# Filter quarters six units sooner with their inputs first, and filter taps formed on two row halves, in a hybrid HGRN2/Hyena layer

## The chip, the cores and the metric

The kernel runs on one core of one Trainium2 chip. The metric is the device time of one execution in microseconds (us). A core has five engines that run their own instruction streams beside each other and meet at semaphores: TensorE (PE), VectorE (DVE), ScalarE (ACT), GpSimd (POOL) and SyncE (SP, here the issuer of most DMAs). The times of the kernel before are 3018.55, 3019.62 and 3019.79 us, median 3019.62 us.

## The reference, cut to what matters

One layer of a diffusion backbone over 256 latent tokens `x` and 256 context tokens, 2048 wide, float32. In this order: a SwiGLU feed-forward network (FFN) for both streams; a mixer, half of it a gated recurrence and half a long two-sided convolution; a second FFN; a final norm. Two preparations stand ahead of the first FFN. The conditioning (`mx`, `mc`: shift, scale and gate vectors) is a product of two vectors with an 18432-column matrix:

```python
mx = [m[:, None, :] for m in jnp.split(jax.nn.silu(c) @ ada_w[l] + ada_b[l], N_MOD, axis=-1)]
mc = jnp.split(jax.nn.silu(c_ctx) @ ada_w[l] + ada_b[l], N_MOD, axis=-1)
x = x + 0.5 * mx[2] * _swiglu(_modulate(_rmsnorm(x, norm_ffn1[l]), mx[0], mx[1]),
                              ffn1_w1[l], ffn1_w3[l], ffn1_w2[l])
```

And the filters of the convolution, from a small network over the 256 positions, through a Fourier transform:

```python
hid = jnp.sin(freq * (z @ w1 + b1))
hid = jnp.sin(freq * (hid @ w2 + b2))
hid = jnp.sin(freq * (hid @ w3 + b3))
h = (hid @ w_out).reshape(n, 2, 2, HY_WIDTH)
...
h = h * jnp.exp(-t[:, None] * deltas)[:, None, None, :]
h_fwd = h[:, :, 0]
h_bwd = h[1:, :, 1]
l1 = jnp.sum(jnp.abs(h_fwd), axis=0) + jnp.sum(jnp.abs(h_bwd), axis=0)
filt = jnp.concatenate([h_fwd, jnp.zeros((1, 2, HY_WIDTH), F32), h_bwd[::-1]], axis=0) / l1
return jnp.fft.rfft(filt, axis=0)
```

The transform needs only the sum and the difference of the forward and the backward taps.

## The kernel before

Weights of the FFNs, the mixer and the output projection stream through in tiles of 128 x 1024 float32 (512 KB). Each is split by ACT (`w_hi`, L431) and DVE (`w_lo`, L438) into two parts, and PE multiplies three times (`three_pass`, L448 to L450). From about 100 us on, this is what the kernel does to its end. The change touches the part ahead of it, which is written out by hand as one loop on each engine over steps `o` from 0 to `TAIL`.

**Conditioning units.** The 4096 columns of `ada_w` that the first norm needs are fetched as 64 units of 128 x 1024 (`load_wide`, L698) on SP's queue. PE takes unit `o` in step `o` with two narrow matmuls (`unit`, L1354: two of the four 32-column strips of the array; the next unit has the other two). Each unit lands in a place of the list `LAND`; the load of a later unit into that place waits until PE has taken the earlier one (`cond_used`). The first 40 units have 16 places, units 40 to 63 have six. In between, SP loads the context tokens `yin`, the decay `window`, the transform `dft` and, at the units of `FIRST_LOADS_AT`, the first FFN weight tiles (L406).

**The filter.** Three layers of the small network are at steps `LAYER_AT` (PE, L1329; seven DVE operations L2089 to L2107; the sine on ACT, L1704). Then come four quarters of 512 filter channels, started at the steps `SPEC_AT`. A quarter goes: POOL's queue loads `fout`, the forward weights on rows 0 to 63 and the backward weights on rows 64 to 127 (L1230); `raw_taps` makes sum and difference for 128 positions at a time (L1381), each as one matmul over all 128 rows, from `hid_sum` and from `hid_dif`, which is `hid_sum` with the sign of its first half turned by `signs`; DVE multiplies by the window (L2124); `spectra` transforms (L1402); ACT and DVE fold even and odd parts (L1735, L2131, L2133) and ACT's queue writes 512 KB twice (`spill`, L1740); `absolute`, `tabs_sum`, `l1_norm` (L1393) and `inverse` make the L1 norm.

**The tokens.** `tokens` turns x and the context with matmuls against the identity (L1340), ACT copies them (L1709) and squares them for the norm. `to_columns` (L1367) and `take` finish a set of 16 units; after the second, DVE and ACT make the FFN's input, one block of 128 columns at a time (`scaled1`, `low1`, L521 and L532; L552), from step `MOD_FIRST` on.

**The opening of the FFN.** After step `TAIL - 1` the first weight tile's matmuls begin (`col_unit`). Its tile has four groups `k` of six matmuls; `inside(j, k)` puts the remaining units 48 to 63 between the groups of tiles `j` = 0 to 3, and the last `l1_norm` and two `to_columns` as well.

Line numbers are those of the kernel before.

Of the kernel before, what the change touches and what calls it, by code (L numbers as in the profile page):

```python
# [23 lines left out]
P = 128  # L24
# [62 lines left out]
SPEC_AT = (10, 18, 28, 36)  # L87
# [9 lines left out]
def shape_tables():  # L97
# [25 lines left out]
    window = blocks(np.exp(-tt[:, None] * deltas)[by_parity]).astype(np.float32)  # L123
# [32 lines left out]
def build(nc, i, out):  # L156
    with ExitStack() as life:
# [64 lines left out]
        fout = sb("fout", [P, 512], scope=first)  # L222
        hid = [sq_sum[:, n * SEQ:(n + 1) * SEQ] for n in range(2)]
        hid_sum = sb("hid_sum", [P, SEQ], scope=first)
        hid_dif = sb("hid_dif", [P, SEQ], scope=first)
        hid.append(hid_sum[:])
# [429 lines left out]
        FIRST_LOADS_AT = (39, 41, 45, 50, 56, 62)  # L656
# [559 lines left out]
        def _(po):  # L1216
# [7 lines left out]
            def filter_out(q):  # L1224
                filt, half = q // 2, q % 2
                if q:
                    po.wait_ge(fs_taps_pe, 4 * q)
                for r in range(2):
                    c0 = filt * (2 * HY) + r * HY + half * 512
                    po.dma_start(fout[r * FILT_ORDER:(r + 1) * FILT_ORDER, :], i["filt_w_out"][0][:, c0:c0 + 512]).then_inc(fs_in, 16)  # L1230

            filter_out(0)
            for q in range(1, 4):
                filter_out(q)

# [44 lines left out]
        MLP_SMALL = 16 * 11  # L1280
# [4 lines left out]
        SQUARES_AT, SUM_AT, ROOT_AT, DIAG_AT, NORM_AT, SPREAD_AT = (5, 5, 7, 7, 11, 11, 12, 12), 14, 14, 15, 24, 25  # L1285
# [4 lines left out]
        WINDOW_AT = ((11, 13), (19, 21), (29, 31), (37, 38))  # L1290
# [1280 lines left out]
```

## Time and profile before

| | us |
|---|---|
| median of three runs | 3019.62 |
| profiled execution, its own time | 3019.63 |
| its span (first to last instruction) | 3017.8 |
| PE busy in the span | 2969.1 |
| DVE busy | 2049.1 |
| ACT busy | 1160.7 |
| POOL busy | 147.7 |
| start of the first FFN matmul | 101.97 |

The profile is of one execution. Times in its rows count from the start of the span, and 1.8 us of the execution lie outside the span. A busy time is the time in which an engine had an instruction running; a wait is the idle time in front of an instruction, with what ended it behind `<-`. PEclk is the granted TensorE clock, 1.00 at the upper of its two levels (2.4 GHz), 0.50 at the lower (1.2 GHz). A row of the timeline with x8 is eight records of one kind in a row: a float32 matmul leaves two, so a pair of units leaves eight and a single unit four.

### The profile page before, as it was taken

The page shows a single profiled execution, that of the slowest core. Times are in us where ns is not written, and L with a number is a line of the kernel's source. Part 1 is how long each engine was busy: PE and PEld are TensorE (multiplying, and loading weights), DVE is VectorE, ACT ScalarE, POOL GpSimd, SP SyncE. Part 2 cuts the span into 40 slices and gives each one's busy share as a digit, 9 for nine tenths or more (in the row PEclk, how much of TensorE's full clock was granted, in tenths as well). Part 3 has the DMA queues.
Part 4 walks back from the last instruction along what each step waited for, and adds up shares of the span by engine and source line. Part 5 has one row for each costly group of instructions (what it writes and reads, how often), then busy time and mean ns, then how long its engine had stood idle before and what let it go on. Part 6 is the DMA issues. An engine that isn't in the chain of part 4 may idle for free. (4 is left out here: it accounts for less than half of the span.)

```text
span 3017.8 us, 42600 instructions
## 1 busy us (share of the span) xinstructions
PE 2969.1 (98%) x15878; PEld 2528.7 (84%) x15878; DVE 2049.1 (68%) x2663; ACT 1160.7 (38%) x1477; POOL 147.7 (5%) x181
## 2 busy tenths in 40 slices
PE   7999999999999999999999999999999999999998
PEld 3588888888888888888889999999998888888886
DVE  4598667676766677673477767778866666666667
ACT  4332222222222222222248777754345444444444
POOL 1000000000000000000000033430000000000001
PEclk9999999999999999999999999999999999999999
DMA  9965546354466758563345554555565666666664
GB/s 370 327 209 188 181 134 202 128 178 146 157 221 221 255 168 282 186 228 102 95 98 167 171 166 148 153 152 180 158 203 168 188 192 190 188 193 189 189 193 147
DMA packets 369856, 559.07 MB, mean 185 GB/s; under 512 B 18175, under 2 KB 260216, under 8 KB 368840
## 3 DMA queue, kind: packets, MB, share of 16 engines
q1 hardware_dynamic: 364112, 544.62, 56.6%
q0 software_dynamic: 2640, 8.52, 0.9%
q10 hardware_dynamic: 2984, 4.29, 0.4%
q8 instruction: 80, 1.31, 0.2%
q14 instruction: 40, 0.33, 0.0%
HBM read 551.06 MB, written 6.30 MB: 185 GB/s over the span
## 5 line engine op out<-in xcount | busy, mean ns | idle before, releaser
L438 DVE TENSOR_TENSOR w_lo<-raw,w_hi 128x1024 fp32r<-128x1024 f32 x736 | 912.6, 1242 | 677.4 <-ACT w_hi L431 675.9
L431 ACT ACTIVATE w_hi<-raw 128x1024 fp32r<-128x1024 f32 x736 | 777.5, 1059 | 1484.2 <-PE bank L450 1093.6
L684 DVE SCALAR_TENSOR_TENSOR states<-ada_raw,silu_c,states 128x1024 f32<-128x1024 f32 x300 | 375.4, 1280 | 2.3
L448 PE MATMUL bank<-h_hi_early,w_hi 128*128 128x512 f32 x768 | 300.7, 391 | 1.0 <-issue 1.0
L450 PE MATMUL bank<-h_hi_early,w_lo 128*128 128x512 f32 x768 | 298.9, 389 | 0.0
L449 PE MATMUL bank<-h_lo_early,w_hi 128*128 128x512 f32 x768 | 298.8, 389 | 0.0
L448 PE MATMUL bank<-hx_hi,w_hi 128*128 128x256 f32 x1024 | 295.2, 288 | 0.0
L450 PE MATMUL bank<-hx_hi,w_lo 128*128 128x256 f32 x1024 | 289.6, 283 | 0.0
L449 PE MATMUL bank<-hx_lo,w_hi 128*128 128x256 f32 x1024 | 289.6, 283 | 0.0
L454 PE MATMUL bank<-w_hi,h 128*128 128x512 f32 x736 | 287.7, 391 | 1.9 <-DVE h L532 1.3
L456 PE MATMUL bank<-w_lo,h 128*128 128x512 f32 x736 | 286.5, 389 | 0.0
L455 PE MATMUL bank<-w_hi,h 128*128 128x512 f32 x736 | 286.4, 389 | 0.0
L448 PE MATMUL bank<-h_hi_late,w_hi 128*128 128x512 f32 x704 | 274.0, 389 | 0.0
L450 PE MATMUL bank<-h_hi_late,w_lo 128*128 128x512 f32 x704 | 273.9, 389 | 0.0
L449 PE MATMUL bank<-h_lo_late,w_hi 128*128 128x512 f32 x704 | 273.9, 389 | 0.0
L448 PE MATMUL bank<-g_hi,w_hi 128*128 128x512 f32 x640 | 249.1, 389 | 0.0
L450 PE MATMUL bank<-g_hi,w_lo 128*128 128x512 f32 x640 | 249.0, 389 | 0.0
L449 PE MATMUL bank<-g_lo,w_hi 128*128 128x512 f32 x640 | 249.0, 389 | 0.0
L449 PEld LDWEIGHTS bank<-hx_lo,w_hi 128*128 128x128 f32 x1024 | 196.3, 192 | 0.2
L448 PEld LDWEIGHTS bank<-hx_hi,w_hi 128*128 128x128 f32 x1024 | 196.2, 192 | 0.2
L450 PEld LDWEIGHTS bank<-hx_hi,w_lo 128*128 128x128 f32 x1024 | 196.1, 191 | 0.0
L1007 DVE SCALAR_TENSOR_TENSOR x_res<-bank,gate,x_res 128x256 f32<-128x256 f32 x176 | 84.8, 482 | 147.7 <-PE bank L450 147.4
(341 smaller groups left out, 4815.0 us busy)
## 6 DMA issues: line engine op xcount, KB each, us to landing
raw<-in_ffn_w_dram SPq DMA_DIRECT2D x528, 512.0 KB, 4.1
ada_raw<-in_ada_w_dram SPq DMA_DIRECT2D x252, 512.0 KB, 4.5
raw<-in_w_in_dram SPq DMA_DIRECT2D x176, 512.0 KB, 3.8
raw<-in_w_out_dram SPq DMA_DIRECT2D x32, 512.0 KB, 3.6
ada_ahead<-in_ada_w_dram SPq DMA_DIRECT2D x20, 512.0 KB, 16.3
raw<-in_ada_w_dram SPq DMA_DIRECT2D x8, 512.0 KB, 18.7
ada_more<-in_ada_w_dram SPq DMA_DIRECT2D x8, 512.0 KB, 8.0
spec<-spec_spill POOLq DMA_DIRECT2D x8, 512.0 KB, 4.0
```

The source lines that it names most:

```text
L431: nc.scalar.activation(w_hi[un.slot(j)][:], raw[un.slot(j)][:], ACT.Copy).then_inc(hi_done, 1)
L438: nc.vector.tensor_tensor(w_lo[un.slot(j)][:], raw[un.slot(j)][:], w_hi[un.slot(j)][:].bitcast(F32), ALU.subtract).then_inc(lo_done, 1)
L448: nc.tensor.matmul(o, w_hi[slot][:, c0:c0 + P], hi, start=start, stop=False, skip_group_check=True)
L449: nc.tensor.matmul(o, w_hi[slot][:, c0:c0 + P], lo, start=False, stop=False, skip_group_check=True)
L450: return nc.tensor.matmul(o, w_lo[slot][:, c0:c0 + P], hi, start=False, stop=stop, skip_group_check=True)
L454: nc.tensor.matmul(o, hi, w_hi[slot][:, c0:c0 + 512], start=start, stop=False, skip_group_check=True)
L455: nc.tensor.matmul(o, lo, w_hi[slot][:, c0:c0 + 512], start=False, stop=False, skip_group_check=True)
L456: return nc.tensor.matmul(o, hi, w_lo[slot][:, c0:c0 + 512], start=False, stop=stop, skip_group_check=True)
L684: nc.vector.scalar_tensor_tensor(out=total, in0=src, scalar=silu_c[:, m, t:t + 1], in1=total, op0=ALU.mult, op1=ALU.add).then_inc(done, 1)
L1007: ins = nc.vector.scalar_tensor_tensor(out=part[:, d, :], in0=bank[downs[d % len(downs)]][:, t * 256:(t + 1) * 256], scalar=gate[:, gt, d, ...
```

## The change

1. `SPEC_AT` goes from (10, 18, 28, 36) to (4, 14, 22, 30). All follow-up steps of a quarter now stand at fixed distances from it. The three layers go from steps 2, 4, 8 to -4, -2 and 1, so the first two stand ahead of unit 0. The tokens of x go to steps 0 and 1, those of the context to 12 and 13.
2. On SP's queue the inputs of the first layers (`emb`, `fw1`, and the three parts of `fw23`, till now on ACT's queue) go ahead of `xin`; `window` and `dft` go behind unit 1, and `yin` behind unit 9.
3. `TAIL` goes from 48 to 44: the FFN opens behind unit 43, and 20 units stand inside it (`INSIDE`), two more pairs between the groups of the first two tiles. `MOD_FIRST` goes from 37 to 35, and the FFN's first weight loads from units (39, 41, 45, 50, 56, 62) to (36, 40, 45, 51, 56, 61). The last `l1_norm` goes from inside the FFN to step 38.
4. POOL loads both halves of a quarter's weights on rows 0 to 63 (`fout_raw`) and makes their sum on rows 0 to 63 of `fout` and their difference on rows 64 to 127. `raw_taps` multiplies the sum by the upper and the difference by the lower 64 rows of one `hid_sum`: two matmuls of 64 rows each in place of two of 128. `signs` goes. The window's first row is halved on the host's table, and DVE makes the one position that has no backward tap with two operations on one partition per quarter.

```diff
-SPEC_AT = (10, 18, 28, 36)
+SPEC_AT = (4, 14, 22, 30)
...
-    window = blocks(np.exp(-tt[:, None] * deltas)[by_parity]).astype(np.float32)
+    decay = np.exp(-tt[:, None] * deltas)
+    decay[0] *= 0.5
+    window = blocks(decay[by_parity]).astype(np.float32)
...
-        FIRST_LOADS_AT = (39, 41, 45, 50, 56, 62)
+        FIRST_LOADS_AT = (36, 40, 45, 51, 56, 61)
...
+            sy.dma_start(emb[:], i["t_emb"]).then_inc(c_in, 16)
+            sy.dma_start(fw1[:], i["filt_w1"][0]).then_inc(c_in, 16)
+            sy.dma_start(fw23[:, 0, :], i["filt_w2"][0]).then_inc(mlp_in, 16)
+            for r in range(2):
+                sy.dma_start(fw23[:, 1 + r, :], i["filt_w3"][0]).then_inc(mlp_in, 16)
             sy.dma_start(xin[:], i["x"][0].rearrange("(a p) d -> p a d", p=P)).then_inc(x_in, 16)
-            for g in range(4):
-                load_wide(sy, g)
-            sy.dma_start(yin[:], i["ctx"][0].rearrange("(a p) d -> p a d", p=P)).then_inc(y_in, 16)
-            for g in range(4, 8):
+            for g in range(2):
                 load_wide(sy, g)
             sy.dma_start(window[:].rearrange("p a c -> p (a c)"), i["t_window"]).then_inc(window_in, 16)
             sy.dma_start(dft[:], i["t_dft"]).then_inc(window_in, 16)
-            for g in range(8, 10):
+            for g in range(2, 10):
                 load_wide(sy, g)
+            sy.dma_start(yin[:], i["ctx"][0].rearrange("(a p) d -> p a d", p=P)).then_inc(y_in, 16)
...
+            def both_ways(q):
+                po.wait_ge(fs_in, 32 * (q + 1))
+                po.wait_ge(*((fs_taps_pe, 4 * q) if q else (memsets, 4)))
+                nc.gpsimd.tensor_tensor(fout[0:FILT_ORDER, :], fout_raw[:, 0, :], fout_raw[:, 1, :], ALU.add).then_inc(fs_hid, 1)
+                po.wait_ge(fs_hid, 2 * q + 1)
+                nc.gpsimd.tensor_tensor(fout[FILT_ORDER:P, :], fout_raw[:, 1, :], fout_raw[:, 0, :], ALU.subtract).then_inc(fs_hid, 1)
...
-        LAYER_AT, ANGLES_AT, SINE_AT = (2, 4, 8), (2, 4, 8), (4, 7, 11)
-        TOKENS_AT, EVICT_AT = (4, 4, 6, 6, 8, 8, 10, 10), (4, 4, 6, 6, 8, 8, 10, 10)
+        LAYER_AT, ANGLES_AT, SINE_AT = (-4, -2, 1), (-4, -2, 1), (-3, -1, 2)
+        TOKENS_AT, EVICT_AT = (0, 0, 1, 1, 12, 12, 13, 13), (0, 0, 1, 1, 12, 12, 13, 13)
...
-        TAIL = 48
-        L1_AT, INVERSE_AT = (20, 28, 37), (21, 29, 38)
...
-        MOD_FIRST = 37
-        FIRST_ROUND_AT = (41, 43, 45)
...
+        TAIL = 44
+        L1_AT, INVERSE_AT = (12, 22, 30, 38), (13, 23, 31, 39)
+        MOD_FIRST = 35
+        FIRST_ROUND_AT = (39, 41, 43)
+        INSIDE = {(0, 0): 44, (0, 1): 46, (0, 2): 48, (1, 0): 50, (1, 1): 52, (1, 2): 54, (2, 0): 56, (2, 2): 58, (3, 0): 60, (3, 2): 62}
...
-                pe.wait_ge(fs_in, 32 * (q + 1))
-                pe.wait_ge(fs_hid, 3)
-                for n, both in enumerate((hid_sum, hid_dif)):
-                    nc.tensor.matmul(bank[2 * a + n][:], both[:, a * P:(a + 1) * P], fout[:], start=True, stop=True
+                    pe.wait_ge(fs_taps, 6 * q)
+                pe.wait_ge(fs_hid, 2 * q + 2)
+                for n in range(2):
+                    own = slice(n * FILT_ORDER, (n + 1) * FILT_ORDER)
+                    nc.tensor.matmul(bank[2 * a + n][:], hid_sum[own, a * P:(a + 1) * P], fout[own, :], start=True, stop=True
...
+                if a == 0:
+                    ve.wait_ge(fs_taps, 6 * q + 2)
+                    nc.vector.tensor_tensor(tsum[0:1, 0, :], tsum[0:1, 0, :], tdif[0:1, 0, :], ALU.subtract).then_inc(fs_taps, 1)
+                    ve.wait_ge(fs_taps, 6 * q + 3)
+                    nc.vector.tensor_scalar(tdif[0:1, 0, :], tsum[0:1, 0, :], -1.0, None, ALU.mult).then_inc(fs_taps, 1)
```

SP's queue, from the third load of the program on; `rows` and `ident` are small inputs, `fw` the layers' weights, L698 and L700 the conditioning units. Before:

```order
L1161 DMA ident<-in_t_ident_dram 128x128
L1162 DMA xin<-in_x_dram 128x2x2048
L698 DMA ada_raw<-in_ada_w_dram 128x1024 x4
L1165 DMA yin<-in_ctx_dram 128x2x2048
L698 DMA raw<-in_ada_w_dram 128x1024 x4
L1168 DMA window<-in_t_window_dram 128x2048
L1169 DMA dft<-in_t_dft_dram 128x512
```

Now:

```order
L1163 DMA ident<-in_t_ident_dram 128x128
L1164 DMA emb<-in_t_emb_dram 33x256
L1165 DMA fw<-in_filt_w_dram 33x64
L1166 DMA fw<-in_filt_w_dram 64x64
L1168 DMA fw<-in_filt_w_dram 64x64 x2
L1169 DMA xin<-in_x_dram 128x2x2048
L700 DMA ada_raw<-in_ada_w_dram 128x1024 x2
L1172 DMA window<-in_t_window_dram 128x2048
L1173 DMA dft<-in_t_dft_dram 128x512
L700 DMA ada_raw<-in_ada_w_dram 128x1024 x2
```

Five small loads stand between `ident` and `xin`; `yin` follows eight units later.

PE at the opening of the FFN (L1354 and L1360 are the units, four rows a pair; L448 to L450, now L450 to L452, the matmuls of a group, of which the first three stand here). Before, from unit 44 on:

```order
L1354 MATMUL bank<-ada_more,c_wide 32x512 x4
L1354 MATMUL bank<-ada_raw,c_wide 32x512 x4
L448 MATMUL bank<-h_hi_early,w_hi 128x512
L449 MATMUL bank<-h_lo_early,w_hi 128x512
L450 MATMUL bank<-h_hi_early,w_lo 128x512
...
L1354 MATMUL bank<-ada_raw,c_wide 32x512 x4
```

Now, from unit 40 on:

```order
L1360 MATMUL bank<-ada_raw,c_wide 32x512 x8
L450 MATMUL bank<-h_hi_early,w_hi 128x512
L451 MATMUL bank<-h_lo_early,w_hi 128x512
L452 MATMUL bank<-h_hi_early,w_lo 128x512
...
L1360 MATMUL bank<-ada_more,c_wide 32x512 x4
```

Units 44 and 45 (`ada_more`) stood two pairs ahead of the first group and now stand behind it; 46 and 47 follow behind the second.

PE around the first filter quarter (L1381 and L1387 are its taps, L1340 and L1346 the tokens, L1329 and L1333 the layers). Before:

```order
L1354 MATMUL bank<-ada_raw,c_wide 32x512 x4
L1329 MATMUL bank<-emb,fw 64x256
L1354 MATMUL bank<-ada_raw,c_wide 32x512 x4
L1329 MATMUL bank<-sq_sum,fw 64x256
L1340 MATMUL bank<-ident,xin 128x128 x16
```

Now:

```order
L1333 MATMUL bank<-emb,fw 64x256
L1333 MATMUL bank<-sq_sum,fw 64x256
L1346 MATMUL bank<-ident,xin 128x128 x16
L1360 MATMUL bank<-ada_raw,c_wide 32x512 x2
L1333 MATMUL bank<-sq_sum,fw 128x256
L1346 MATMUL bank<-ident,xin 128x128 x16
L1360 MATMUL bank<-ada_raw,c_wide 32x512 x6
L1387 MATMUL bank<-fout,sq_sum 128x512 x2
```

The first two layers now stand ahead of every unit, and the first taps (the last row) behind four units instead of ten.

## Rows read from the trace of the kernel before

**Rows 1.** Busy time in the span, the page's first part.
```profile
PE 2969.1 (98%) x15878; PEld 2528.7 (84%) x15878; DVE 2049.1 (68%) x2663; ACT 1160.7 (38%) x1477; POOL 147.7 (5%) x181
```

**Rows 2.** Stretches: length, busy of each engine, granted clock, DMA share, GB/s.
```profile
60.00:80.00 20.00, 20.00 (x98) 7.48 (x99) 12.09 (x44) 6.99 (x9) 1.67 (x4) 1.00 1.04 377
80.00:100.00 20.00, 17.14 (x77) 5.01 (x77) 17.48 (x35) 7.53 (x16) 0.00 (x0) 1.00 1.04 395
100.00:120.00 20.00, 18.41 (x94) 10.26 (x94) 12.16 (x23) 8.33 (x12) 0.00 (x0) 1.00 1.03 396
140.00:160.00 20.00, 20.00 (x94) 16.67 (x93) 18.34 (x41) 9.91 (x19) 0.00 (x0) 1.00 0.43 147
```

**Rows 3.** PE timeline, first 40 us: start, length, form, idle before.
```profile
18.36 1.11 PE L1329 MATMUL bank<-emb,fw 33*64 33x256 f32 x2 [0.58 <-DMA fw<-in_filt_w_dram]
28.21 1.97 PE L1340 MATMUL bank<-ident,xin 128*128 128x128 f32 x16
35.23 1.06 PE L1354 MATMUL bank<-ada_ahead,c_wide 128*32 128x512 f32 x8
```

**Rows 4.** PE timeline, 40 to 102 us.
```profile
40.19 1.84 PE L1381 MATMUL bank<-fout,hid_sum 128*128 128x512 f32 x2 [1.99 <-DVE hid_dif L2114]
...
44.71 1.12 PE L1381 MATMUL bank<-fout,hid_sum 128*128 128x512 f32 x2
...
46.62 1.06 PE L1354 MATMUL bank<-ada_ahead,c_wide 128*32 128x512 f32 x8
47.62 1.98 PE L1402 MATMUL bank<-tsum,dft 128*128 128x512 f32 x4
49.53 1.06 PE L1354 MATMUL bank<-ada_ahead,c_wide 128*32 128x512 f32 x8
...
99.56 1.05 PE L1354 MATMUL bank<-ada_raw,c_wide 128*32 128x512 f32 x4 [1.71 <-DMA ada_raw<-in_ada_w_dram]
```

**Rows 5.** PE timeline, opening of the FFN.
```profile
101.97 0.50 PE L448 MATMUL bank<-h_hi_early,w_hi 128*128 128x512 f32 x1
...
103.56 1.05 PE L1354 MATMUL bank<-ada_raw,c_wide 128*32 128x512 f32 x4
...
109.84 1.06 PE L1354 MATMUL bank<-ada_more,c_wide 128*32 128x512 f32 x8 [1.00 <-DMA ada_more<-in_ada_w_dram]
...
115.71 0.50 PE L448 MATMUL bank<-h_hi_early,w_hi 128*128 128x512 f32 x1
...
117.22 0.95 PE L1367 MATMUL bank<-pairs,states 128*128 128x4 f32 x8
```

**Rows 6.** SP's queue: issue time and length of the issue.
```profile
1.68 0.41 SPq L1161 DMA_DIRECT2D ident<-in_t_ident_dram  x1
2.13 0.43 SPq L1162 DMA_DIRECT2D xin<-in_x_dram  x1
...
81.97 0.94 SPq L698 DMA_DIRECT2D ada_raw<-in_ada_w_dram  x2
...
102.08 0.33 SPq L698 DMA_DIRECT2D ada_raw<-in_ada_w_dram  x1
```

**Rows 7.** Issues at 82 us, at 102 us, and the spills: KB, median us to landing.
```profile
ada_raw<-in_ada_w_dram SPq DMA_DIRECT2D x2, 512.0 KB, 11.3
...
ada_raw<-in_ada_w_dram SPq DMA_DIRECT2D x1, 512.0 KB, 10.3
...
spec_spill<-spec_cos ACTq DMA_DIRECT2D x4, 512.0 KB, 8.1
```

**Rows 8.** Stretches, columns as in the second group: near the start; two at lower clock.
```profile
3.00:4.00 1.00, 0.16 (x1) 0.16 (x1) 0.00 (x0) 0.00 (x0) 1.00 (x3) 1.00 0.76 137
5.00:6.00 1.00, 0.00 (x0) 0.00 (x0) 0.00 (x0) 0.00 (x0) 1.00 (x3) 1.00 0.94 385
40.40:43.80 3.40, 3.40 (x8) 0.86 (x11) 0.71 (x2) 3.38 (x7) 0.00 (x0) 0.50 1.04 413
1560.00:1570.00 10.00, 7.50 (x50) 7.53 (x51) 9.66 (x22) 6.65 (x13) 0.00 (x0) 0.83 0.23 61
```

**Rows 9.** DVE and POOL operations of the quarters' shape.
```profile
L2139 DVE TENSOR_TENSOR tabs<-tabs x4: 692/692/693, 52.9 to 108.9; 128x512 f32<-128x512 f32 x4
...
L1276 POOL TENSOR_TENSOR xt<-x_tok,norm_row 128x512 f32<-128x512 f32 x7 | 10.9, 1552 | 798.2 <-DVE x_tok L1033 798.2
```

More of the change, by code:

```diff
@@ L222, in build @@
         fout = sb("fout", [P, 512], scope=first)
+        fout_raw = sb("fout_raw", [FILT_ORDER, 2, 512], scope=first)
         hid = [sq_sum[:, n * SEQ:(n + 1) * SEQ] for n in range(2)]
-        hid_sum = sb("hid_sum", [P, SEQ], scope=first)
-        hid_dif = sb("hid_dif", [P, SEQ], scope=first)
-        hid.append(hid_sum[:])
+        hid_sum = hid[0]
+        hid.append(hid_sum)
         ada_more = [sb(f"ada_more{n}", [P, UNIT], scope=first) for n in range(2)]
@@ L1226, in filter_out @@
                 if q:
-                    po.wait_ge(fs_taps_pe, 4 * q)
+                    po.wait_ge(fs_hid, 2 * q)
                 for r in range(2):
                     c0 = filt * (2 * HY) + r * HY + half * 512
-                    po.dma_start(fout[r * FILT_ORDER:(r + 1) * FILT_ORDER, :], i["filt_w_out"][0][:, c0:c0 + 512]).then_inc(fs_in, 16)
-            filter_out(0)
-            for q in range(1, 4):
+                    po.dma_start(fout_raw[:, r, :], i["filt_w_out"][0][:, c0:c0 + 512]).then_inc(fs_in, 16)
+            def both_ways(q):
[4 more added lines that the diff above has]
+                nc.gpsimd.tensor_tensor(fout[FILT_ORDER:P, :], fout_raw[:, 1, :], fout_raw[:, 0, :], ALU.subtract).then_inc(fs_hid, 1)
+            for q in range(4):
                 filter_out(q)
+                both_ways(q)
             po.wait_ge(mod_done, 12)
@@ L1314, in turn @@
             def turn(n, after):
-                pe.wait_ge(after, 48 if n == 3 else SMALL)
+                pe.wait_ge(after, 80 if n == 3 else SMALL)
                 if n < 3:
@@ L1336, in tokens @@
                     pe.wait_ge(tr_out, g - 3)
+                if g == 8:
+                    pe.wait_ge(fs_out, 4)
                 for k in range(2):
@@ L1406, in _ @@
             pe.wait_ge(memsets, 3)
-            for o in range(TAIL):
+            for o in range(LAYER_AT[0], TAIL):
                 if o in LAYER_AT:
@@ L1430, in _ @@
                     l1_norm(L1_AT.index(o))
-                unit(o)
+                if o >= 0:
+                    unit(o)
             def inside(j, k):
-                g = TAIL + 4 * j + k
-                if k in (0, 2) and g < ADA_UNITS:
-                    unit(g)
-                    unit(g + 1)
-                if (j, k) == (0, 3):
-                    l1_norm(3)
+                if (j, k) in INSIDE:
+                    unit(INSIDE[j, k])
+                    unit(INSIDE[j, k] + 1)
                 if (j, k) == (1, 1):
@@ L1691, in _ @@
                                  ).then_inc(mlp_in, 16)
-            ac.dma_start(fw23[:, 0, :], i["filt_w2"][0]).then_inc(mlp_in, 16)
-            for r in range(2):
-                ac.dma_start(fw23[:, 1 + r, :], i["filt_w3"][0]).then_inc(mlp_in, 16)
             ac.wait_ge(cols_done, 1)
@@ L1715, in square_tokens @@
                 if n >= 2:
-                    ac.wait_ge(n1["sq"], n - 1)
-                nc.scalar.activation((sq2 if n % 2 else xn2)[:], src, ACT.Square, accum_out=tok_sq[:, n:n + 1]).then_inc(n1["sq"], 1)
+                    ac.wait_ge(n1["sq"], n if n >= 4 else n - 1)
+                nc.scalar.activation((sq2 if n in (1, 3) else xn2)[:], src, ACT.Square, accum_out=tok_sq[:, n:n + 1]
+                                     ).then_inc(n1["sq"], 1)
             def row_out(nth):
@@ L1740, in spill @@
                 ac.dma_start(dst, spec_out[o][:]).then_inc(fs_dma[o], 16)
-            for o in range(TAIL):
+            for o in range(LAYER_AT[0], TAIL):
                 if o in SINE_AT:
@@ L2169, in scaled1 @@
                 scaled(ve, n1, 0, [x_res, y_res], (0, 1), kb)
-            for o in range(TAIL):
+            for o in range(LAYER_AT[0], TAIL):
                 if o in ANGLES_AT:
@@ L2180, in _ @@
                     lanes()
-                if o == SPEC_AT[0]:
-                    signs()
                 if o in TAKE_AT:
```

62 lines of the change are left out of this document (21 added, 41 removed).

## The prediction, written before the changed kernel was run

> **What bounds the kernel now.** I read the busy times first. PE has an instruction running in 2969.1 of 3017.8 us [rows 1], so the end moves only by what PE's waits or its work lose or gain. Then the stretches. From 140 us on PE is busy throughout and the DMA engines have spare time (share 0.43); from 60 to 120 us the DMA share is full and PE nearly so [rows 2]. The reader is to see two nearly equal bounds side by side there: PE's instruction stream and the stream of loads. The PE timeline tells which one ends last. Up to 95 us PE takes units long after they have landed. From unit 44 on it waits for them: 1.71 us before unit 46, and inside the FFN once more, 1.00 us before units 50 and 51, which landed at 109.8 [rows 4, 5]. So the opening of the FFN is set by PE's earlier work up to 95 us, and by the stream just behind it. SP's queue comes last: units 42 and 43 are issued at 82 us and take 11.3 us to land, at about 94; unit 53 is issued at 102.08 and takes 10.3, to 112.4 [rows 6, 7]. A full queue stands in front of each, so bandwidth and not the issue sets these times.
>
> The profiled execution took 3019.63 us, as good as the median of 3019.62. The sum is made on it.
>
> **What PE saves.** Eight calls of `raw_taps`: with the clock up, one call holds PE from 44.71 to 46.62, 1.91 us, for two matmuls of the full height [rows 4]. On two row halves with two banks they can run side by side, 0.95 us a call: 7.6 us. If they don't, 0. The nearest row for the better end is the pair of units: four matmuls on four column strips take 1.0 us (46.62 to 47.62), about as long as one unit alone (four records, 1.05 us) [rows 4], so the array does run strips at once. I take 0.95.
>
> The Trainium skill (TensorEngine Tiling (Array Packing), Key Properties) says that row tiles work in parallel, but also that each change of the tiling mode drains TensorE, and now two kinds of tiling alternate with full-height work. The trace agrees that this is cheap: the pair of units and the full-height transform alternate at 1.00 and 1.91 us without a gap. By the rule a drain would be paid as before, since units and taps differed in mode already.
>
> The earlier start saves more. The first layer waited until 18.9 us for its weights, then the tokens and three layers followed, and the first taps began at 40.19 behind a wait of 1.99 for the signs [rows 3, 4]. In the new order the first taps stand behind four units and need only x.
>
> **When PE could open the FFN.** Put the context tokens as PE's new start. They stand behind unit 11. In front of that in the stream stand x, 12 units, window, dft and yin, the same bytes as before in front of unit 11; unit 9 was taken as it landed at 35.2 [rows 3], so unit 11 about 2.6 later, 37.8. With the shift worked out below 39.3, and one unit more, 40. From there to the FFN PE has: tokens 2 x 1.97, 32 units at 0.5 (16.0), six calls of taps (5.7), six transforms at 1.91 (11.5), four `l1_norm`, two `to_columns` and the norm at 1.0 (7), together 44: ready at 84. Without the side by side 90. DVE's two added operations on one partition have at most the length of a full one, 0.69 us [rows 9]: 1.4 a quarter, 5.5 in all, less 0.6 for `signs`. They lie between taps and transform; if nothing covers them PE is ready 4 us later, 88 (94). POOL's two operations have 64 rows; for 128 rows of the same length one took 1.55 [rows 9], so 3.1 a quarter at most. Behind the last taps of a quarter follow at least six units and two transforms, 6.8 us, before the next taps: covered. For the first quarter nobody waits before 25 us.
>
> **When the stream opens it.** Five small loads stand in front of `xin` now. Successive issues there are 0.45 us apart (1.68, 2.13) [rows 6], so x is issued up to 2.25 later. Before, the engines were partly used in that time (0.76 in the fourth microsecond, 0.94 in the sixth) [rows 8], and the small loads fall into it, moved from ACT's queue. Bounds of the shift: 0 and 2.25; I take 1.5, nearer the upper, since x is most of what ran there. From then on the engines are full until past 110, and the shift stays. In front of unit 43 stand two FFN loads, as before; but the last quarter's two spills of 512 KB now come in front of it as well. At 395 GB/s [rows 2] that is 1.33 each, 2.7. Unit 43 lands at 94.1 + 1.5 + 2.7 = 98.3, and a unit takes 1.0: the FFN opens at 99.3. PE would be ready at 84 to 94, so the stream decides, and the 7.6 us of the taps become waiting.
>
> **Inside the FFN.** A group takes 1.4 us, 1.6 behind a unit (101.97 to 103.56) [rows 5]. Up to unit 53 there are now six groups and five pairs: 9.2 + 5.0 = 14.2, which gives 113.5. But unit 53 lands at 112.4 + 1.5 = 113.9 (all spills and as many FFN loads, four, stand in front of it in both kernels), so its matmuls end at 114.95. What comes next is `to_columns`, in both kernels behind six groups and unit 53; it stood at 117.22 [rows 5]. `l1_norm` has been done on both sides. Gain 117.22 - 114.95 = 2.27 us. From there the order is the same in both, the later units landed more than 2.3 us ahead of their use, and PE had no wait up to 160 but one: the gain goes through to the end. 3019.63 - 2.3 = 3017.3 us.
>
> So of 7.6 us saved in matmuls and more than 10 in an earlier start, 2.3 arrive.
>
> **Rivals.**
>
> A. The stream isn't shifted, or runs denser because PE frees its places sooner. For: the small loads fill a gap that was there. Against: share 1.04 between 80 and 120 already [rows 2]. Unit 53 at 112.4 gives 117.22 - 113.45 = 3.8: 3015.8. A stream that is also 1.5 us denser gives 5.3: 3014.3.
>
> B. The lower clock. PE is now idle for about a third of the time between 40 and 98. Before, the idle 1.99 us at 38 to 40 was followed by 3.4 us at clock 0.50 [rows 4, 8], in which taps took 3.5 instead of 1.9. If such a stretch falls on the first groups of the FFN, half of its work, 1.7 us, is lost: 3019.0. While PE only waits for units it costs nothing.
> The Trainium skill (TensorE: Matmul & The Clock Gate, Part 1) says that the lower clock is the default and only activity releases it; by this rule more waiting means more such stretches, and the sum with one is the 3019.0 just worked out.
> Further on there are such stretches too, as at 1560 to 1570 with mean 0.83 [rows 8]; each holds 1.7 us, and whether short waits there bring one may change with any shift, to both sides.
>
> C. Slower: PE is the bound after all. Place: the hand-overs of a quarter, PE taps, DVE window, PE transform, ACT, DVE, PE's next taps. The taps that covered DVE's work are halved and DVE has 1.4 us more. It decides from an opening of the FFN at 117.22 - 14.2 = 103.0 on, and each microsecond later costs one. Against: PE's 84 leaves 19 us, and the loop before ran from 44 to 95 without a wait. With 24 hand-overs (three quarters of eight) of 1 us each it is 108: 3024.6.
>
> D. The row halves don't run side by side. For: no row shows row halves. PE is ready at 90 to 94, still before 98: the time stays 3017.3. This rival shows only in the spacing of the taps, and I give it a fifth of the chance of the forecast.
>
> E. The loads in front of x hold the stream more than issue time, because x's packets queue behind many tiny ones. From a shift of 3.8 on the kernel is slower; 5 would give 3020.8.
>
> **Chances.** Forecast, D included: 0.60. A 0.17 (of it 0.05 beyond 0.2%, with a later low-clock stretch gone as well: 3014.3 - 1.7 = 3012.6). B 0.12. C 0.07, of it 0.05 slower by over 0.2%. E 0.04, of it 0.02. A measurement of this kernel tells 0.2%, 6.0 us, from no change; 2.3 us lies within. So faster 0.05, within 0.88, slower 0.07. The forecast's own range is 3015.8 (shift 0) to 3019.0 (one low-clock stretch); the range for 8 in 10 goes to A's denser stream, 3014.2, and to E's 3020.8.
>
> **What would show it.** Right: first taps at about 25 us; a call of taps in about 1 us; waits of PE for units all along 45 to 98, 10 us or more in sum; the FFN opening at 99 +- 2 behind a load, with short waits for units inside; `to_columns` of the third set at about 115; the same from 140 on, shifted. Wrong: if PE's waits before the FFN name DVE or ACT, it is C; if x lands later than 14.5, E; if unit 53 is taken well before 112, A's stream is denser than I believe; if the difference arises behind 160 us, none of this is the cause.

## The result, and the profile after

The changed kernel takes 3028.53 us (median of 8 runs, 3025.61 to 3031.68) against 3019.70 (3017.82 to 3020.23) for the kernel before on the same chip: ratio 1.0031, 95% interval 1.0021 to 1.0040. It is slower by 8.8 us. 3017.3 was forecast, in a range up to 3020.8. The profiled run took 3025.61, the lowest of the eight, and its span is 6.0 us longer than before's, so the rows show 6.0 of the 8.8 us.

The page's first part has PE's own work smaller, as intended: 2965.1 us where [rows 1] has 2969.1. The span grew all the same.

```profile
span 3023.8 us, 42617 instructions
PE 2965.1 (98%) x15878; PEld 2526.5 (84%) x15878; DVE 2052.1 (68%) x2668; ACT 1162.3 (38%) x1477; POOL 157.8 (5%) x189
```

The stretches that answer to [rows 2], same columns:

```profile
60.00:80.00 20.00, 15.21 (x58) 5.80 (x58) 11.87 (x46) 4.77 (x8) 0.14 (x1) 0.80 0.95 359
80.00:100.00 20.00, 19.86 (x98) 6.32 (x96) 13.19 (x26) 7.48 (x11) 2.53 (x2) 0.95 0.70 244
100.00:120.00 20.00, 14.93 (x79) 6.63 (x80) 17.95 (x37) 9.89 (x19) 0.00 (x0) 0.91 1.03 398
140.00:160.00 20.00, 20.00 (x99) 15.16 (x92) 11.77 (x26) 8.41 (x15) 0.00 (x0) 1.00 0.61 202
```

PE idles 4.8 of 20 us from 60 to 80, where it had no gap; its clock is at 0.80 there; and from 80 to 100 the stream of loads, full before, has a share of 0.70. The PE timeline names the waits (answers to [rows 3 to 5]; L1387 taps, L1360 units, L1346 tokens, L1406 transforms, L1372 `to_columns`, L1397 `l1_norm`, L1424 the norm):

```profile
24.84 1.13 PE L1387 MATMUL bank<-fout,sq_sum 64*128 64x512 f32 x4
...
42.80 1.94 PE L1360 MATMUL bank<-ada_ahead,c_wide 128*32 128x512 f32 x8 [6.30 <-DMA ada_ahead<-in_ada_w_dram]
44.67 3.56 PE L1346 MATMUL bank<-ident,yin 128*128 128x128 f32 x16
...
52.81 1.13 PE L1387 MATMUL bank<-fout,sq_sum 64*128 64x512 f32 x4
53.87 1.06 PE L1360 MATMUL bank<-ada_ahead,c_wide 128*32 128x512 f32 x8
...
61.04 1.35 PE L1372 MATMUL bank<-pairs,states 128*128 128x4 f32 x8 [4.05 <-ACT states L1721]
62.26 3.34 PE L1406 MATMUL bank<-tsum,dft 128*128 128x512 f32 x4
...
76.29 2.08 PE L1424 MATMUL bank<-xn,ones_d 128*128 128x512 f32 x2 [3.75 <-DVE hy_cols L2143]
...
101.59 1.05 PE L1397 MATMUL bank<-pairs,tabs 128*128 128x1 f32 x8 [1.73 <-DVE tabs L2135]
...
104.28 3.31 PE L1360 MATMUL bank<-ada_raw,c_wide 128*32 128x512 f32 x16
111.07 0.47 PE L450 MATMUL bank<-h_hi_early,w_hi 128*128 128x512 f32 x1 [3.48 <-issue]
...
125.38 1.05 PE L1372 MATMUL bank<-pairs,states 128*128 128x4 f32 x8
```

Read it from the top. The first taps stand at 24.84 instead of 40.19 [rows 4], and a call of taps holds PE 1.06 us (52.81 to 53.87) instead of 1.91. Then PE waits for ACT, for DVE, for DVE, and the FFN opens at 111.07 instead of 101.97 [rows 5]. The third `to_columns` stands at 125.38 instead of 117.22, 8.2 us later. From 140 on PE is busy without a gap as before.

Why ACT was late at 61.04: its rows from 56 us on (L1714 squares of the context, L1755 the root, L1752 the Exp of the bounds, L1721 `row_out`).

```profile
56.30 1.06 ACT L1714 ACTIVATE xn<-yin 128x1024 f32<-128x1024 f32 x1
57.26 0.19 ACT L1714 ACTIVATION_READ_ACCUMULATOR xn<-yin 128x1 f32 x1
57.46 1.28 ACT L1755 ACT_TABLE_LOAD   x1
58.76 0.20 ACT L1755 ACTIVATE pairs<-pairs 128x4 f32<-128x4 f32 x1
58.98 1.28 ACT L1752 ACT_TABLE_LOAD   x1
60.27 0.23 ACT L1752 ACTIVATE lbe<-lbe 128x32 f32<-128x32 f32 x1
60.41 0.58 ACT L1721 ACTIVATE states<-bank 128x512 f32<-128x512 f32 x1
```

`row_out` needs only unit 15, done at 54.9. It stands in ACT's order behind four squares of the context (the first starts at 52.55, when the tokens are out; they last to 57.46) and behind two table loads. In the kernel before the same squares ran from 39.16 to 43.45, long ahead of it:

```profile
52.17 0.60 ACT L1723 ACTIVATE states<-bank 128x512 f32<-128x512 f32 x1 [0.39 <-issue]
```

The DVE timeline has the same twice (L2182 the sum of the squares, L2115 the window products, L2058 to L2053 the bounds and lane sums, L2143 the end of `inverse`, L440 `w_lo`):

```profile
57.48 0.16 DVE L2182 TENSOR_TENSOR pairs<-pairs 128x4 f32<-128x4 f32 x1 [8.19 <-ACT xn L1714]
57.56 0.69 DVE L2115 TENSOR_TENSOR tsum<-bank,window 128x512 f32<-128x512 f32 x1
...
70.91 0.17 DVE L2058 TENSOR_TENSOR lbt<-lbe 128x16 f32<-128x16 f32 x1
...
73.54 0.20 DVE L2053 COPY same_lane<-same_lane 128x64 f32<-128x64 f32 x1
73.65 0.68 DVE L2115 TENSOR_TENSOR tsum<-bank,window 128x512 f32<-128x512 f32 x1
...
76.12 0.12 DVE L2143 TENSOR_TENSOR hy_cols<-bank,cols 128x4 f32<-128x4 f32 x1
...
109.75 1.22 DVE L440 TENSOR_TENSOR w_lo<-raw,w_hi 128x1024 fp32r<-128x1024 f32 x1
```

The first taps of the second quarter were done at 53.9; their window products stand behind a sum that waits for ACT, and start at 57.56. From 70.91 to 73.65 24 small operations, 2.7 us, stand ahead of the third quarter's products and of the `inverse` that the norm waits for. At the end the first `w_lo` stands behind the chain of `h_lo` parts; it ends at 110.97, and the first FFN matmul waits for it (the 3.48 us that the row calls `issue`). PE's late progress also holds up the loads. SP's issues (start, length):

```profile
5.78 0.61 SPq L1169 DMA_DIRECT2D xin<-in_x_dram  x1
...
57.02 10.41 SPq L700 DMA_DIRECT2D ada_raw<-in_ada_w_dram  x4
85.17 0.33 SPq L700 DMA_DIRECT2D ada_ahead<-in_ada_w_dram  x1
```

Between 67.4 and 85.2 SP issues nothing: the next unit's place is free only when PE has taken the unit before it in that place. No wait of PE between 44.67 and the opening names a load, so no row shows that this gap cost time.

### The profile page after: what moved, and what is told of

It is laid out like the page before. It is cut to its first block and busy times, and to the rows that moved or that the text cites. A ratio compares the mean times of both kernels' runs of the same rounds, so it can differ in the third digit from the quotient of the medians.

```text
span 3023.8 us, 42617 instructions
## 1 busy us (share of the span) xinstructions
PE 2965.1 (98%) x15878; PEld 2526.5 (84%) x15878; DVE 2052.1 (68%) x2668; ACT 1162.3 (38%) x1477; POOL 157.8 (5%) x189
## 5 line engine op out<-in xcount | busy, mean ns | idle before, releaser
L440 DVE TENSOR_TENSOR w_lo<-raw,w_hi 128x1024 fp32r<-128x1024 f32 x736 | 912.4, 1242 | 678.1 <-ACT w_hi L433 675.7
L450 PE MATMUL bank<-h_hi_early,w_hi 128*128 128x512 f32 x768 | 300.6, 391 | 4.5 <-issue 4.5
L452 PE MATMUL bank<-h_hi_early,w_lo 128*128 128x512 f32 x768 | 298.9, 389 | 0.0
L450 PE MATMUL bank<-hx_hi,w_hi 128*128 128x256 f32 x1024 | 295.2, 288 | 0.0
L452 PE MATMUL bank<-hx_hi,w_lo 128*128 128x256 f32 x1024 | 289.6, 283 | 0.0
L450 PE MATMUL bank<-h_hi_late,w_hi 128*128 128x512 f32 x704 | 274.0, 389 | 0.0
L452 PE MATMUL bank<-h_hi_late,w_lo 128*128 128x512 f32 x704 | 273.9, 389 | 0.0
L450 PE MATMUL bank<-g_hi,w_hi 128*128 128x512 f32 x640 | 249.1, 389 | 0.0
L452 PE MATMUL bank<-g_hi,w_lo 128*128 128x512 f32 x640 | 249.0, 389 | 0.0
L450 PEld LDWEIGHTS bank<-hx_hi,w_hi 128*128 128x128 f32 x1024 | 196.2, 192 | 0.2
L452 PEld LDWEIGHTS bank<-hx_hi,w_lo 128*128 128x128 f32 x1024 | 196.1, 191 | 0.0
```

The source lines that it names most:

```text
L440: nc.vector.tensor_tensor(w_lo[un.slot(j)][:], raw[un.slot(j)][:], w_hi[un.slot(j)][:].bitcast(F32), ALU.subtract).then_inc(lo_done, 1)
L450: nc.tensor.matmul(o, w_hi[slot][:, c0:c0 + P], hi, start=start, stop=False, skip_group_check=True)
L452: return nc.tensor.matmul(o, w_lo[slot][:, c0:c0 + P], hi, start=False, stop=stop, skip_group_check=True)
```

## The experiments

Beside each changed kernel the kernel before ran on the same chip; ratios are to it, with their 95% intervals. Not all experiments ran on one chip, so they are compared by these ratios.

**Row halves alone, steps as before.** The kernel before, with `fout_raw`, `both_ways`, the row halves in `raw_taps` and the two one-partition operations.

> The kernel before with the row halves, GpSimd's additions and the halved window row alone (part 4), all steps and the load order as before. Theory H (hand-overs, lower clock and the recycled places of the units make PE late in the changed kernel; the row halves are harmless): the eight calls of taps shrink from 1.91 to about 1.05 us, PE reaches the last units sooner and waits there for the stream, which ended last by about 3 us in sum, so 0 to 3 us faster than before: 3016.7 to 3019.7. Rival R (the row halves or GpSimd's additions are the cause): most of the 9 us appears here, 3024 or more. Rival S (the load order is the cause): no change, 3019.7.

3019.65 us, ratio 1.0002 (0.9993 to 1.0012): no change. PE timeline:

```profile
66.80 1.06 PE L1363 MATMUL bank<-ada_ahead,c_wide 128*32 128x512 f32 x8 [2.33 <-DMA ada_ahead<-in_ada_w_dram]
...
97.48 1.06 PE L1363 MATMUL bank<-ada_more,c_wide 128*32 128x512 f32 x8 [0.84 <-DMA ada_more<-in_ada_w_dram]
100.19 3.16 PE L1363 MATMUL bank<-ada_raw,c_wide 128*32 128x512 f32 x8 [1.64 <-DMA ada_raw<-in_ada_w_dram]
103.28 0.56 PE L450 MATMUL bank<-h_hi_early,w_hi 128*128 128x512 f32 x1
```

The time saved in the taps turns into waits for units, and part of it into the lower clock (100.19: a pair of units in 3.16 us). GpSimd's sums cost nothing that the time shows. So the loss lies in the other part.

**The new steps alone.** The changed kernel with full-height taps, `hid_dif` and `signs`.

> The changed kernel with full-height taps from two copies of the last layer's output, as before (parts 1 to 3 without part 4). H: as late as the changed kernel or later, since the taps take 7.6 us more of PE, part of it where PE waits anyway: 3027 to 3034. R: back to the kernel before, 3018 to 3021. S: as the changed kernel, 3028.5.

3029.38 us, ratio 1.0034 (1.0022 to 1.0047): the whole loss. PE waits 2.33 us for `states`, 1.59 for `hy_cols` and 1.73 for `tabs`, and opens the FFN at 110.16. Halving the taps buys 0.0003 of the ratio here, within both intervals. With full-height taps to cover DVE's work and without DVE's two operations the same three waits stand there, two of them shorter: neither the shorter taps nor these operations are the cause of the loss.

**The context stream sooner.**

```diff
-            for g in range(2, 10):
+            for g in range(2, 4):
                 load_wide(sy, g)
             sy.dma_start(yin[:], ...)
+            for g in range(4, 10):
+                load_wide(sy, g)
```

> The changed kernel with the context tokens loaded behind unit 3, as before, instead of behind unit 9; all else as changed. H: the wait for units 10 and 11 stays, since the same bytes stand in front of unit 11; PE still starts the context tokens at step 12, so 0 to 2 us less than the changed kernel: 3026.5 to 3028.5. S (the late context holds everything up): the opening of the FFN comes back by 5 us or more, 3023 or less. R: no change.

3030.82 us, ratio 1.0037 (1.0023 to 1.0051): no cure. The wait for loads moves to 33.19 (7.16 us), the others stay (4.05 for `states`, 3.41 for `hy_cols`), and the FFN opens at 113.10. The place of the context's load is not the cause.

**The context's squares, sums and root later.**

```diff
-        SQUARES_AT, SUM_AT, ROOT_AT, DIAG_AT, ... = (2, 3, 3, 4, 13, 14, 14, 15), 15, 15, 16, ...
+        SQUARES_AT, SUM_AT, ROOT_AT, DIAG_AT, ... = (2, 3, 3, 4, 17, 18, 19, 20), 21, 21, 21, ...
-                if o == 16:
+                if o == 20:
                     ac.wait_ge(lb_dve, 3)
```

> The changed kernel with ScalarE's squares of the context moved from steps 13 to 15 to steps 17 to 20 and the token sums, root and reciprocals from 15 and 16 to 21, behind the first row of sums (step 17) and VectorE's window products of the second quarter. H: PE's wait of 4.05 us for ScalarE's row goes, and VectorE no longer holds the window products for 8 us; PE reaches step 26 about 4 us sooner, the places come free sooner: 3022 to 3026, 4 us less than the changed kernel. S and R: no change, 3028.5.

3025.44 us, ratio 1.0021 (1.0011 to 1.0030). The Exp of the bounds moved with them, as the second part of the edit shows. The wait for `states` is gone, but the next one grew:

```profile
72.84 2.08 PE L1424 MATMUL bank<-xn,ones_d 128*128 128x512 f32 x2 [5.82 <-DVE hy_cols L2143]
```

PE came there sooner (65.96 instead of 71.48 for the unit ahead of it) and DVE did not.

**DVE's small operations later as well.** On top of the last one; the norm one step later with it. (By the rows they are 24 in 2.7 us, not 30 in 3.7 as the expectation has it.)

```diff
-... = (2, 3, 3, 4, 17, 18, 19, 20), 21, 21, 21, 24, 25
+... = (2, 3, 3, 4, 17, 18, 19, 20), 21, 21, 21, 25, 26
-                if o == 22:
+                if o == 26:
                     bounds_rest()
                     lanes()
```

> The kernel of the run with the context's squares later, and besides DVE's 30 small operations of the bounds and the lane sums (3.7 us) four steps later, into a gap of DVE, and the norm's matmul one step later. Theory H (hand-overs): the wait of 5.8 us that PE had there for hy_cols goes, the low clock behind it too, 4 to 6 us sooner at the first FFN group (103 or less, against 107.8), time 3020 to 3022. Rival S (the stream decides): PE's wait comes back as a wait for units, the FFN opens at 106 or later, time 3024 to 3026.

3020.01 us, ratio 1.0004 (0.9995 to 1.0013). Some 8 of the 8.8 us are back with no matmul, load or sum changed; only places in ACT's and DVE's order moved. The wait of 5.82 is 1.30, and

```profile
102.25 0.65 PE L450 MATMUL bank<-h_hi_early,w_hi 128*128 128x512 f32 x1 [3.00 <-issue]
...
118.05 1.05 PE L1372 MATMUL bank<-pairs,states 128*128 128x4 f32 x8
```

**DVE's small operations alone.** The changed kernel with only that second step.

> The changed kernel with DVE's 30 small operations four steps later and the norm's matmul one step later, the context's squares left where they are. Theory H: the wait of 2.1 us for hy_cols and the low clock behind it go, the wait for states (4.05) stays; time 3023 to 3026. Rival (only the two together help, or ACT's queue is the whole cause): within 1 us of the changed kernel, 3027 to 3029.

3022.82 us, ratio 1.0012 (1.0003 to 1.0021), better than expected. The wait for `hy_cols` is gone, the one for `states` (4.05 at 61.00) stays, the FFN opens at 107.00. The norm's matmul moved one step with the operations, and its share is not separated. By the ratios the squares alone take 0.0010 off the 0.0031, the small operations alone 0.0019, both 0.0027. Each ratio is good to about 0.001, so this shows two blockings that each cost time, and fits with their adding up, without proving it.

**Matmuls that keep PE busy in its waits.** On the kernel with both moves; their results are not used.

```diff
+            def fill(b, count):
+                for _ in range(count):
+                    nc.tensor.matmul(bank[b][:, 384:512], ident[:], ident[:], start=True, stop=True, ...)
...
+                if 4 <= o < 13:
+                    fill(7, 4)
```

and `fill(5, 4)` ahead of the norm and of the last `l1_norm`, `fill(5, 12)` ahead of the FFN.

> The same as the run before it in this call, with matmuls of the identity added for PE where it had been waiting: four in front of units 4 to 12, four in front of the norm and in front of the last l1_norm, twelve in front of the FFN (their results are not used). Theory H with the clock as a cost of its own: the low-clock stretches between 40 and 110 us go or shrink to one, the time is 2 to 4 us below the kernel without them. Rival (the clock matters only where PE waits anyway, or the added matmuls cost what they save): within 1 us of it or slower.

3020.95 us, ratio 1.0006 (0.9997 to 1.0015). No stretch at the lower clock is left before 1566 us (40 to 60 has clock 1.00 where it had 0.83). But four added matmuls hold PE 1.09 us where nothing covers them, and the FFN opens at 105.05. They cost what they saved: inconclusive on the price of the clock.

**The old steps, the FFN four units sooner.** The kernel with the row halves alone, with `TAIL = 44`, `MOD_FIRST = 35`, `FIRST_ROUND_AT = (39, 41, 43)`, the new `INSIDE` and `FIRST_LOADS_AT`, the last quarter's `absolute` at 41 and 42, its spills at 41 and 43 and its tabs at 43.

> The old order of the filter steps, with the row halves and GpSimd's sums as in the run with the halves alone, and of the new order only what lies at the end: the FFN opens behind unit 43 instead of 47, loads of its first weights some units sooner. Theory H: the waits for loads of that run (2.5 us before the opening, 1.4 behind it) become FFN work; opening at 99 to 101 or where DVE's parts of h are ready (102), third to_columns at 115 to 116.5, time 3015 to 3018. Rival: DVE is late with the parts of h, opening later than 103, 3019 or more.

3022.96 us, ratio 1.0014 (1.0005 to 1.0023): the rival. The loads no longer hold PE at the opening; DVE does, 4.14 us for `tsum` at 92.32 and 4.48 for `sq` at 104.10, since the modulation now stands ahead of the last quarter in its order.

**The small loads behind x.** On the kernel with both moves.

```diff
+            sy.dma_start(xin[:], ...).then_inc(x_in, 16)
             sy.dma_start(emb[:], i["t_emb"]).then_inc(c_in, 16)
...
-            sy.dma_start(xin[:], ...).then_inc(x_in, 16)
```

> As the run with the bounds later, with the five small loads of the filter network behind x instead of in front of it. Theory S, E of the prediction: x lands near 12.2 instead of 14.0, units up to 10 some 2 to 4 us sooner, the FFN opens 2 or more us sooner, time 2 to 4 us less than that run. Theory H: PE's later hand-overs decide, the first layers start later instead, time within 1 us of it.

3019.21 us, ratio 0.9999 (0.9990 to 1.0008). PE takes units 10 and 11 at 42.86 instead of 44.08, and opens the FFN at 102.18 instead of 102.25: of what the loads in front of x cost, 1.2 us is back at unit 10, and with DVE's order deciding at the opening none of it arrives there.

**The first `w_lo` sooner, the last quarter's tabs later.** On top of that.

```diff
-        FIRST_ROUND_AT = (39, 41, 43)
+        FIRST_ROUND_AT = (37, 41, 43)
+                if (j, k) == (0, 3):
+                    l1_norm(3)
             def early_lo(j):
+                if j == 0:
+                    tabs_sum(3)
+                    inverse(3)
```

> The kernel with x in front, and two more moves on DVE: the first unit's w_lo two steps sooner, in front of part of the h_lo chain, and the last quarter's tabs, l1_norm and inverse behind the opening of the FFN. In that kernel PE was ready at 98.9 and the FFN opened at 102.2, as w_lo ended. Theory H (PE waits for DVE's instruction order): the FFN opens at 97 to 100, the third to_columns stands at 115 to 117 instead of 118.0, time 3017 to 3018.5. Rival S (the stream): the units inside the FFN are waited for by as much, to_columns stays at 117 or later, time 3019.

3025.72 us, ratio 1.0021 (1.0012 to 1.0030): by the ratios 6.6 us slower than without. The opening did what was expected, and then (PE, and DVE below it):

```profile
98.58 0.50 PE L450 MATMUL bank<-h_hi_early,w_hi 128*128 128x512 f32 x1
...
115.56 1.87 PE L1397 MATMUL bank<-pairs,tabs 128*128 128x1 f32 x8 [5.61 <-DVE tabs L2137]
```

```profile
112.42 1.22 DVE L440 TENSOR_TENSOR w_lo<-raw,w_hi 128x1024 fp32r<-128x1024 f32 x1 [5.56 <-ACT w_hi L433]
113.56 1.22 DVE L2135 TENSOR_TENSOR tabs<-tabs,tabs_dif 128x1024 f32<-128x1024 f32 x1
```

DVE stood idle for 5.56 us in front of the fourth unit's `w_lo`, with the tabs behind it in its order: the mistake of this change made once more, by hand.

**The context stream behind unit 11**, and **the same with matmuls in the waits for loads** (`fill(7, 4)` in front of units 5, 6, 10, 11, `fill(7, 8)` in front of the context's tokens). Both on that kernel.

> The kernel before it in this call, with the context stream loaded behind unit 11 instead of unit 9. PE waits for units 10 and 11 behind it now, and takes them when the context could already be transposed. Theory H: the two units are taken in the wait, the context's tokens start 1 to 2 us sooner, and what follows up to 90 us as well; at the opening little is left of it (DVE or the stream decide): time within 1 us of the kernel before it. Rival: it goes through to the end, 1 to 2 us less.

> The same with matmuls of the identity (not used) only where PE waits for loads anyway: four in front of units 5, 6, 10 and 11, eight in front of the context's tokens. Theory H with the clock as a cost: no low-clock stretch between 40 and 50 us, the context's tokens at full clock and PE 2 to 3 us sooner behind them; at the end 0 to 2 us. Rival (the clock costs nothing there): the same within 1 us in every row from 50 us on.

3025.06 us, ratio 1.0021 (1.0012 to 1.0030), and 3025.49, ratio 1.0022 (1.0013 to 1.0031). Both share the wait for tabs, behind which nothing of what they do can show. Ahead of it the rows answer. With the context behind unit 11 its tokens start at 42.40 instead of 44.93, but in a stretch at clock 0.50 from 41.2 to 51.6, and the second quarter's first taps stand at 53.27 instead of 52.53. With the added matmuls no stretch at 0.50 stands before 115 us, and the same taps stand at 53.87. So keeping the clock up did not bring PE forward, and the rival of the second expectation came true.

**The tabs ahead of the fourth `w_lo`.** One call of `tabs_sum(3)` moved, nothing else.

```diff
+            tabs_sum(3)
+
             def early_lo(j):
                 if j == 0:
-                    tabs_sum(3)
                     inverse(3)
```

> The kernel with the first w_lo two steps sooner, with the last quarter's tabs between the h_lo chain and the fourth unit's w_lo instead of behind that one, whose load lands at 111. Theory H with the stream as the next bound (the prediction's own sum): the FFN opens at 98 to 99, no wait for tabs, the third to_columns behind unit 53 at 114.5 to 116.5 against 117.2 in the kernel before the change, time 3016 to 3018. Rival: DVE's chain of h_lo parts or the tabs hold the FFN's groups up, to_columns at 118 or later, 3019.5 or more.

3017.89 us (11 runs, 3016.09 to 3018.76), before 3019.55; ratio 0.9995 (0.9985 to 1.0004). PE and DVE:

```profile
94.50 1.05 PE L1360 MATMUL bank<-ada_raw,c_wide 128*32 128x512 f32 x4 [2.01 <-DMA ada_raw<-in_ada_w_dram]
96.43 3.38 PE L1360 MATMUL bank<-ada_raw,c_wide 128*32 128x512 f32 x8 [0.89 <-DMA ada_raw<-in_ada_w_dram]
99.75 0.80 PE L450 MATMUL bank<-h_hi_early,w_hi 128*128 128x512 f32 x1
...
110.78 0.95 PE L1397 MATMUL bank<-pairs,tabs 128*128 128x1 f32 x8
...
116.72 1.05 PE L1372 MATMUL bank<-pairs,states 128*128 128x4 f32 x8
```

```profile
107.29 1.22 DVE L2135 TENSOR_TENSOR tabs<-tabs,tabs_dif 128x1024 f32<-128x1024 f32 x1
...
113.40 1.23 DVE L440 TENSOR_TENSOR w_lo<-raw,w_hi 128x1024 fp32r<-128x1024 f32 x1 [4.17 <-ACT w_hi L433]
```

7.8 us for the place of two DVE instructions of 1.9 us in sum. Ahead of the opening PE waits for loads alone now. The time is still not told from the kernel before.

**The same with the later context stream and the added matmuls.**

> The same with the context stream behind unit 11 and the matmuls of the identity in PE's waits for loads before 50 us (not used). If the lower clock costs time by itself, PE is 1 to 3 us sooner at 60 us and the end comes up to 2 us sooner than without; if the stream decides at 98 and 115 again, rows from 98 on agree within 1 us and so does the time.

3017.69 us, ratio 0.9996 (0.9987 to 1.0005). No lower clock before 1563 us, where the run before has two stretches of 6.8 us (at 41.0 and 95.6); PE at 50 us is no sooner (added matmuls until 47.2); and

```profile
99.34 0.50 PE L450 MATMUL bank<-h_hi_early,w_hi 128*128 128x512 f32 x1
...
117.21 1.05 PE L1372 MATMUL bank<-pairs,states 128*128 128x4 f32 x8
```

agree within 0.5 us. Here, with waits for loads right ahead of the opening in both, removing the lower clock gained nothing at the end.

## Why the prediction was wrong

**The step that failed is "When PE could open the FFN".** It added PE's own work behind the context's tokens, 44 us, and let nothing but a possible 4 us of DVE's extra operations stand in it: PE ready at 84, or 94 at worst. Measured from the same point to the end of unit 43, it took 62.9 us (44.67 to 107.59). The rows divide the 18.9 us too many so: 9.5 are waits for ACT and DVE (4.05, 3.75, 1.73), 8.0 is what the clock at 0.50 took from PE's work behind these waits and behind the one for loads (tokens in 3.56 us instead of 1.97, a transform in 3.34, four units in 3.31), and about 1.4 is the rest, above all two units taken singly at 1.0 us and taps at 1.06. Behind unit 43 came 3.48 more for the first `w_lo`, for which the sum had no term. With the later start (44.67 instead of 40) the whole is 40 + 4.7 + 62.9 + 3.5 = 111.1, the opening. The waits of 4.05 and 3.75 and the one for `w_lo` are shown by experiment: moving the blocking instructions takes them away, and of the first two the time as well. The 1.73 stayed in every kernel with the tabs at this step and no added matmuls. The 8.0 us is arithmetic on rows: no run changed the clock alone on the path that decides.

**Why the waits were missed.** The prediction asked of each moved PE step whether its data would be there. It did not ask what else stands ahead in the order of ACT and DVE at the steps where the quarters now fall. The context's squares went from steps 11 and 12 to 13 to 15, right behind tokens that PE now has only at 44 to 52, and `row_out(0)` stayed at 17, two steps behind the last of them: no slack for 4.9 us of squares and 2.6 of table loads is left. `bounds_rest` and `lanes` stayed at 22, where a quarter now begins. Neither piece is in a line of the diff that looks costly; the second is in none at all. At the opening the first `w_lo` stands at the end of DVE work that has no gap from 96.69 to 110.97.

**Rival C was right in kind, and near in its number partly by luck.** It named the hand-overs of a quarter, an opening past 103 as the point from which it decides, 108 as the place and 3024.6 as the time. It opened at 111.07, and the profiled run took 3025.61. "If PE's waits before the FFN name DVE or ACT, it is C": they do. It got 0.07, on the ground that before had no wait from 44 to 95. That row spoke of an order in which other instructions stood at these steps. C was off in two points. The loss is not in 24 hand-overs by 1 us each, but in a few long waits, of which the first is not of a quarter at all, and nearly as much again in the lower clock behind them. And C's reason, taps halved and DVE with 1.4 us more, is refuted by the run with the new steps alone, which has neither and loses the same.

**The shorter taps** were sized right: 1.06 us a call against 0.95, and D is wrong. The Trainium skill (TensorEngine Tiling (Array Packing), Key Properties) says that changing the tiling mode drains TensorE. In this trace a call takes 1.06 us and the pair of units behind it 1.00 (52.81, 53.87, 54.87), with no gap between them: whatever a drain costs here is inside these numbers. That the savings would become waiting is what the run with the row halves alone shows.

**The stream.** The small loads in front of x cost more than the 1.5 us taken. x was issued 3.65 us later (5.78 against 2.13 [rows 6]) because issues there took 0.5 to 0.75 us each instead of 0.45, and its tokens started at 14.08, just short of rival E's 14.5. Stretches of before, then of after (columns as in [rows 2]):

```profile
0.00:5.00 5.00, 0.31 (x1) 0.18 (x1) 0.33 (x3) 0.00 (x0) 4.46 (x15) 1.00 0.39 89
5.00:10.00 5.00, 0.00 (x0) 0.00 (x0) 0.00 (x0) 1.49 (x3) 5.00 (x11) 1.00 0.97 358
```

```profile
0.00:5.00 5.00, 0.00 (x0) 0.00 (x0) 0.00 (x0) 0.15 (x1) 4.46 (x15) 1.00 0.22 44
5.00:10.00 5.00, 1.35 (x3) 0.46 (x3) 2.68 (x9) 1.68 (x4) 5.00 (x11) 1.00 0.68 196
```

In ten microseconds 1.2 MB instead of 2.2 came in (5 x 44 + 5 x 196 against 5 x 89 + 5 x 358 KB), 2.7 us of stream at the 377 GB/s of [rows 2]. Units 10 and 11 were taken as they landed, at 42.80 instead of the 39.3 of the sum, and their pair took 1.87 us behind the wait, so PE came to the context's tokens at 44.67 instead of 40. With the hand-overs mended, the run with these loads behind x took 1.2 us of it back, and none of that reached the end. In the changed kernel itself no wait for a load follows, so there the later start may have counted in full; no run shows it.

**The bounds behind it held roughly, with some luck.** With the hand-overs mended and the tabs moved the FFN opens at 99.75 against 99.3 in the prediction, and the time is 3017.89 against 3017.3. But this kernel loads x in front of the small loads, so the 1.5 us of shift in the sum is not in it, its `l1_norm` stands inside the FFN again, and two errors meet at the opening: unit 43 landed at 97.8, 0.5 sooner than in the sum, and took 1.9 us at the lower clock instead of 1.0. The third `to_columns` stands at 116.72, not 114.95: the groups up to it took 17.0 us instead of 14.2, of which `l1_norm` is 0.9 and the lower clock 1.4. Unit 53 had landed at 114.8 and was taken at 115.73 without a wait, so PE's groups and not the stream set the place. In the changed kernel itself that piece took 14.3 (111.07 to 125.38). So the forecast fits a kernel whose ACT and DVE order has been moved along with PE's, and this one's had not; whether its 2.3 us of gain are real, the interval of 0.9985 to 1.0004 does not tell.

**Behind 160 us** the order is the same and the shift of 8.2 us at `to_columns` goes through, less 2.2: the profiled run has one stretch at the lower clock behind 1500 us (3.4 us long, at 1570) where before had two (1563, 2177), as rival B said could go to either side. The other executions of the changed kernel are up to 6 us slower than the profiled one. Their mean granted clock goes with it: 0.995 in the two at 3025.6 and 3025.7, 0.994 at 3027.25, 0.993 in the five from 3028.4 up. By an estimate from these figures, 0.002 of 3025 us is 6 us, so they had more of the lower clock; where it lay is open, since only the profiled one has a trace.

**Slips in the sum.** The first layer before started at 18.36 after a wait of 0.58 [rows 3], not at 18.9. By the sum's own figures (44 us of work between 40 and 98) PE would be idle for a quarter of that time, not for a third. Neither touches the result.

## What to carry to other kernels

When steps of a static order are moved for one engine, list for each engine that hands over to it what stands ahead of the handed-over instruction at the new place, unmoved instructions too: an in-order engine makes PE wait for whatever is in front, however cheap it is. "No wait in this stretch before" vouches for the old order alone. Where two bounds lie close together (here PE's order and a full stream of loads), shortening one gave nothing, and a few instructions in the wrong place cost eight microseconds, in waits and in the work at the lower clock behind them.

## What the runs showed of the hardware

- Two fp32 matmuls of 64 rows on the two row halves, into different banks, run side by side: the two take 1.06 us where two of 128 rows took 1.91.
- A table load on ACT takes 1.28 us; two of them, for a root of 4 columns and an Exp of 32 (0.20 and 0.23 us), stood on PE's path.
- PE's waits of 3.75 to 7.59 us behind 20 us were each followed by work at clock 0.50, in stretches of 3.4 to 10.4 us; with matmuls in the waits there was no such stretch before 1563 us, or before 115 where the wait for tabs had none. That bought no time in any of three pairs of runs.
- GpSimd adds 64x512 in 1.27 us, two a quarter, and no row shows a wait for it.
